# The first norm's shift and scale made by TensorE in column quarters, beside the first three weight tiles

## The reference, cut to what matters

```python
c_act = jax.nn.silu(c)
mod = (c_act @ w_mod[l] + b_mod[l])[:, None, :]
sh1, sc1, g1, sh2, sc2, g2 = jnp.split(mod, N_MOD, axis=-1)
h = rms_norm(x) * (1.0 + sc1) + sh1
proj = h @ w_in[l]
u, v, z, xbc, dt_raw, gate_a, gate_b = jnp.split(proj, offs, axis=-1)
```

## Time and profile before

| | us |
|---|---|
| three runs, median (lowest to highest) | 1546.25 (1546.24 to 1548.23) |
| the profiled execution, own time | 1547.16 |
| its span | 1545.9 |
| TensorE busy with matmuls | 1468.4 |
| VectorE busy | 875.1 |
| ScalarE busy | 636.5 |
| GpSimd busy | 191.0 |
| DMA: moved in all, and mean rate | 142.87 MB, 92 GB/s |
| mean granted clock of TensorE, share of full | 0.983 |

### The profile page before, as it was taken

How to read it: one execution, slowest core, us unless ns; L and a number is a source line. 1 busy time by engine, 2 the same in 40 slices (tenths; PEclk the granted TensorE clock), 3 DMA queues, 4 the chain that set the end, 5 groups by cost and what they waited for, 6 DMA issues and landing times.

```text
span 1545.9 us, 25397 instructions
## 1 busy us (share of the span) xinstructions
PE 1468.4 (95%) x10113; PEld 1154.8 (75%) x10113; DVE 875.1 (57%) x1222; ACT 636.5 (41%) x980; POOL 191.0 (12%) x230
## 2 busy tenths in 40 slices
PE   5899999999999999899998999999998999999996
PEld 2687777777788878688876888888885676766675
DVE  3577777776635754654546442344347765655745
ACT  3564445444555422332234431233324445353433
POOL 0000000000017788630005000000000000000000
PEclk9899999999999999899998999999998999999998
DMA  9332222223245565443332333333332212111111
GB/s 304 82 96 68 69 72 74 75 69 82 68 121 152 155 172 164 126 119 96 95 96 66 98 96 96 95 96 95 97 112 65 56 43 56 43 42 40 49 40 55
DMA packets 263403, 142.87 MB, mean 92 GB/s; under 512 B 4805, under 2 KB 261882, under 8 KB 263290
## 3 DMA queue, kind: packets, MB, share of 16 engines
q1 hardware_dynamic: 263290, 141.26, 32.2%
HBM read 139.14 MB, written 2.10 MB: 91 GB/s over the span
## 4 chain that ended last, share of the span: by engine, by line
PE 85%; DVE 7%; ACT 4%; issue 3%; DMA 0%; SPq 0%; DVEq 0%; ACTq 0%
PE PS L555 24%; PE PS L557 23%; PE PS L556 23%; PE PS L698 1%; DVE Hl L1647 1%; DVE Ww L2248 1%; PE PS L960 1%; PE PS L944 1%; PE PS L662 1%; PE PS L703 1%; DVE macc L1669 1%; PE PS L682 1%; DVE wlo L1635 1%; PE PS L952 1%; PE PS L849 1%
## 5 line engine op out<-in xcount | busy, mean ns | idle before, releaser
L555 PE MATMUL PS<-Hh,whi 128*128 128x512 f32 x1290 | 545.1, 423 | 18.6 <-DVE wlo L1635 3.7
L557 PE MATMUL PS<-Hh,wlo 128*128 128x512 f32 x1290 | 507.9, 394 | 0.0
L556 PE MATMUL PS<-Hl,whi 128*128 128x512 f32 x1290 | 507.3, 393 | 0.0
L1635 DVE TENSOR_TENSOR wlo<-raw,whi 128x1024 fp32r<-128x1024 f32 (+2 forms) x211 | 273.3, 1295 | 106.2 <-ACT whi L1107 104.9
L555 PEld LDWEIGHTS PS<-Hh,whi 128*128 128x128 f32 x1290 | 244.8, 190 | 92.1 <-issue 30.9
L557 PEld LDWEIGHTS PS<-Hh,wlo 128*128 128x128 f32 x1290 | 244.6, 190 | 53.4
L1107 ACT ACTIVATE whi<-raw 128x1024 fp32r<-128x1024 f32 (+2 forms) x211 | 221.5, 1051 | 151.4 <-PE PS L557 151.3
L556 PEld LDWEIGHTS PS<-Hl,whi 128*128 128x128 f32 x1290 | 245.5, 190 | 47.7 <-issue 6.6
L453 POOL TENSOR_TENSOR mbuf<-mbuf,cact 128x1024 f32<-128x1024 f32 x32 | 62.2, 1942 | 468.1 <-DMA mbuf<-in_w_mod_dram 468.1
L555 PE MATMUL PS<-YBh,whi 128*128 128x512 f32 x256 | 99.6, 389 | 0.0
L556 PE MATMUL PS<-YBl,whi 128*128 128x512 f32 x256 | 99.6, 389 | 0.0
(11 more groups left out here) (401 smaller groups left out, 1721.7 us busy)
## 6 DMA issues: line engine op xcount, KB each, us to landing
raw<-in_w_in_dram SPq DMA_DIRECT2D x106, 512.0 KB, 4.0
raw<-in_w_ff_dram SPq DMA_DIRECT2D x64, 512.0 KB, 4.1
mbuf<-in_w_mod_dram SPq DMA_DIRECT2D x32, 512.0 KB, 4.0
wm<-in_w_mod_dram SPq DMA_DIRECT2D x8, 1024.0 KB, 11.9
raw<-in_w_branch_ssm_dram SPq DMA_DIRECT2D x16, 512.0 KB, 4.2
raw<-in_w_out_dram SPq DMA_DIRECT2D x10, 512.0 KB, 4.1
raw<-in_w_branch_gm_dram SPq DMA_DIRECT2D x8, 512.0 KB, 4.1
raw<-in_w_out_dram SPq DMA_DIRECT2D x6, 448.0 KB, 3.8
```

Source lines behind the costliest of these rows:

```text
L555: pe.matmul(bank[:, :], whi[s][:, k, :], xh[:, kk, :], start=kk == 0, stop=False)
L556: pe.matmul(bank[:, :], whi[s][:, k, :], xl[:, kk, :], start=False, stop=False)
L557: last = pe.matmul(bank[:, :], wlo[s][:, k, :], xh[:, kk, :], start=False, stop=t == end - 1 and k == (order or range(kt))[-1])
L1635: v.tensor_tensor(wlo[s][:, 0:kt, :], raw[s][:, 0:kt, :], whi[s][:, 0:kt, :].bitcast(F32), ALU.subtract).then_inc(s_wlo, 1)
```

## The change

VectorE's part in the product of silu(c) and w_mod goes, and so does the second turn of x. In its place:

- SP loads x0 and x1 ahead of `fill1`, x2 and x3 behind it; then the w_mod pieces in quarters, each a piece of the scale and one of the shift (wm4 and wm0, then wm5 and wm1, and so on), with the first three weight tiles and `fill2` between the quarters. Tiles 3 to 5 are loaded ahead of bc and bsb.
- TensorE turns x chunk by chunk as it lands, into eight banks; VectorE copies it to XT (`x_copy`). The reciprocal root is spread over the partitions by four matmuls (L618 of the changed kernel).
- Each piece is multiplied by eight matmuls that write 32 partitions each, four groups in turn (`mod_rows`), copied by ScalarE (`mod_row`), and summed and turned by two matmuls of one column with `selc`, a column that picks one row of each group (`mod_sums`).
- A quarter gives scale and shift of two slices k: VectorE makes the two columns (`h_cols`), then XT by scale by spread root (`h_scaled`), ScalarE adds the shift and rounds (`h_hi`), VectorE takes the rest (`h_lo`).
- Between the quarters TensorE runs tiles dt, cv0 and cv1 for the slices that are there (`part`), so the three tiles are worked by channels, not one after the other.
- After them tile cv2 comes first in `gemm`. The work of `conv` is one tile later than before: conv(0) runs beside cv2, conv(1) beside cv3, conv(2) and conv(3) beside z0 and z1, both gates beside cv4 (`FIRST`, `after`). `dt_steps` runs from cv2 on, so it has four tiles and a rest, where it had six.

The diff, cut to its core:

```diff
 def sp_program(sp):
-        for to, ap in fill1:
-            sp.dma_start(to, ap).then_inc(s_par, 16)
-        for c in range(NC):
-            sp.dma_start(xnat[:, c, :], ...).then_inc(s_x, 16)
-        for i in range(8):
-            sp.dma_start(wm[i][:, :, :], cols(W_MOD, i * 256, 256)).then_inc(s_wm[i], 16)
-        for t in range(3):
-            load(t)
+        load_x(0)
+        load_x(1)
+        for to, ap in fill1:
+            sp.dma_start(to, ap).then_inc(s_par, 16)
+        load_x(2)
+        load_x(3)
+        load_mod0(0)
+        load(0)
+        load(1)
+        load_mod0(1)
+        load(2)
         for to, ap in fill2:
             sp.dma_start(to, ap).then_inc(s_par2, 16)
+        load_mod0(2)
+        load_mod0(3)
+        for t in range(3, 6):
+            load(t)
         sp.wait_ge(s_pc, 5)
...
 def pe_program(pe):
+        def mod_rows(n):
+            if n >= 3:
+                pe.wait_ge(s_mrow, n - 2)
+            pe.wait_ge(s_wm[MOD0[n]], 16)
             for k in range(KT):
-                tr = pe.matmul(row[0:1, 0:256], cact[:, k:k + 1], wm[i][:, k, :], start=k == 0, stop=k == KT - 1)
+                q = 32 * (k % 4)
+                ms = pe.matmul(BK[3 + n % 3][q:q + 32, 0:256], cact[:, k:k + 1].to_broadcast([P, 32]), wm[MOD0[n]][:, k, :],
+                               start=k < 4, stop=k >= 4)
+            ms.then_inc(s_mt, 1)
+        def mod_sums(n):
+            pe.wait_ge(s_mrow, n + 1)
+            if n >= 2 and n % 2 == 0:
+                pe.wait_ge(s_modc, n)
             for j in range(2):
-                ms = pe.matmul(bk[...], macc[:, j * 128:(j + 1) * 128], ones[:, 0:1],
+                ms = pe.matmul(BK[6][:, 2 * n + j:2 * n + j + 1], mrow[n % 2][:, j * 128:(j + 1) * 128], selc[:, 0:1],
                                start=True, stop=True)
+            ms.then_inc(s_ms, 1)
+        def part(t, *ks):
+            ...
+            for k in ks:
+                pe.wait_ge(s_hi, k + 1)
+                pe.wait_ge(s_lo, k + 1)
+                pe.matmul(bank[:, :], whi[t][:, k, :], Hh[:, k, :], start=k == 0, stop=False)
+                pe.matmul(bank[:, :], whi[t][:, k, :], Hl[:, k, :], start=False, stop=False)
+                last = pe.matmul(bank[:, :], wlo[t][:, k, :], Hh[:, k, :], start=False, stop=k == KT - 1)
+        mod_rows(0)
+        mod_rows(1)
+        mod_sums(0)
+        mod_sums(1)
+        part(0, 0, 1)
+        part(1, 0, 1)
+        mod_rows(2)
+        mod_rows(3)
+        mod_sums(2)
+        mod_sums(3)
+        part(0, 2, 3)
+        part(1, 2, 3)
+        mod_rows(4)
+        mod_rows(5)
+        part(2, 0, 1)
+        mod_sums(4)
+        mod_sums(5)
+        part(2, 2, 3)
+        mod_rows(6)
+        mod_rows(7)
+        part(0, 4, 5)
+        mod_sums(6)
+        mod_sums(7)
+        part(1, 4, 5)
+        part(2, 4, 5)
         pe.wait_ge(s_par2, N_PAR2)
...
+        for t in range(3):
+            part(t, 6, 7)
...
 def dve_program(v):
+        def h_scaled(m):
+            v.wait_ge(s_modc, 2 * (m // 2) + 1)
+            ...
+            v.scalar_tensor_tensor(out=tmp[m % 3][:, :], in0=XT[:, m, :], scalar=opc[:, m:m + 1], in1=BK[7][:, :],
+                                   op0=ALU.mult, op1=ALU.mult).then_inc(s_hb, 1)
+        def h_lo(m):
+            ...
+            v.scalar_tensor_tensor(out=Hl[:, m, :], in0=tmp[m % 3][:, :], scalar=modc[:, m:m + 1],
+                                   in1=Hh[:, m, :].bitcast(F32), op0=ALU.add, op1=ALU.subtract).then_inc(s_lo, 1)
+        for j in range(4):
+            h_cols(j)
+            h_scaled(2 * j)
+            h_scaled(2 * j + 1)
+            if j == 0:
+                lo(0)
+            if j == 1:
+                lo(2)
+            h_lo(2 * j)
+            if j == 0:
+                lo(1)
+            h_lo(2 * j + 1)
...
-        for g in range(8):
+        for name, beside in FIRST:
+            main[0] = after(beside, conv, gate_z)
+            tile_steps(name, KT, 5)
+        main[0] = after([("z", 0), ("z", 1)], conv, gate_z)
+        drain()
+        side[0] = ssd(0)
+        for g in range(1, 8):
```

More of the change, by code:

```diff
@@ L219, in build_program @@
     N_BC, N_WS, N_W2 = N_PAR2 + 64, N_PAR2 + 80, N_PAR2 + 128
[L220 removed]
+    s_const, s_par, s_par2 = sem("s_const"), sem("s_par"), sem("s_par2")
+    s_x = [sem(f"s_xl{c}") for c in range(NC)]
     s_wm = [sem(f"s_wm{i}") for i in range(8)]
@@ L272, in build_program @@
     turn(("dt", 0), s_dta, 1)
+    dtT = BK[5]
+    MOD0 = [i for j in range(4) for i in (4 + j, j)]
     for q in range(32):
@@ L372, in build_program, with after @@
     DT, AA, CU, NCU, EC, WE, EL, SC = (dts[:, i, :] for i in range(8))
+    FIRST = [(("cv", 2), [("cv", 0)]), (("cv", 3), [("cv", 1)]), (("z", 0), [("cv", 2)]), (("z", 1), [("cv", 3)])]
+    def after(names, conv, gate_z):
+        gens = [conv(i) if kind == "cv" else gate_z(i) for kind, i in names]
+        for k in range(KT):
+            for gen in gens:
+                next(gen, DONE)
+            yield
     def sp_program(sp):
@@ L404, in sp_program @@
         mod_after = {tile0[name] + 2: q for q, name in enumerate(MODS)}
-        for t in range(3, NT):
+        for t in range(6, NT):
             load(t)
@@ L563, in gemm, with x_turned @@
             return bank
+        def x_turned(c):
+            pe.wait_ge(s_x[c], 16)
+            for m in range(KT):
+                if c == 2 and m == KT - 1:
+                    pe.wait_ge(s_pc, 3)
+                tr = pe.transpose(BK[m][:, c * 128:(c + 1) * 128], xnat[:, c, m * 128:(m + 1) * 128], ident[:, :])
+                if c == NC - 1:
+                    tr.then_inc(s_xtt, 1)
         pe.wait_ge(s_const, 2)
+        x_turned(0)
+        x_turned(1)
         pe.wait_ge(s_par, 16 * 7)
-        pe.transpose(BK[1][:, :128], pr[1][:, :], ident[:, :]).then_inc(s_pt, 1)
@@ new lines, in pe_program @@
+        x_turned(2)
+        x_turned(3)
+        pe.wait_ge(s_xrs, 1)
+        pe.wait_ge(s_xt0, 1)
+        for c in range(NC):
+            ms = pe.matmul(BK[7][:, c * 128:(c + 1) * 128], small[:, 4 + c:5 + c].to_broadcast([P, P]), ident[:, :],
+                           start=True, stop=True)
+        ms.then_inc(s_xsp, 1)
+        pe.wait_ge(s_cact, 1)
+        pe.wait_ge(s_const, 13)
+        pe.wait_ge(s_xt0, 8)
+        def mod_rows(n):
+            if n >= 3:
+                pe.wait_ge(s_mrow, n - 2)
+            pe.wait_ge(s_wm[MOD0[n]], 16)
+            for k in range(KT):
+                q = 32 * (k % 4)
+                ms = pe.matmul(BK[3 + n % 3][q:q + 32, 0:256], cact[:, k:k + 1].to_broadcast([P, 32]), wm[MOD0[n]][:, k, :],
+                               start=k < 4, stop=k >= 4)
+            ms.then_inc(s_mt, 1)
@@ L727, in pe_program @@
         ALL = range(KT)
-        pe.wait_ge(s_pc, 5)
-        gemm(("dt", 0), Hh, Hl, 0)
         side[0] = dt_steps()
         for g in range(8):
-            for j in range(4):
+            for j in range(0 if g else 2, 4):
                 gemm(("cv", 4 * g + j), Hh, Hl, None, ALL)
@@ L1878, in tile_steps @@
                     slot(name)
-        slot(("dt", 0))
+        slot(("cv", 0))
+        slot(("cv", 1))
         side[0] = dt_steps()
-        for g in range(8):
+        for name, beside in FIRST:
+            main[0] = after(beside, conv, gate_z)
+            tile_steps(name, KT, 5)
+        main[0] = after([("z", 0), ("z", 1)], conv, gate_z)
+        drain()
+        side[0] = ssd(0)
+        for g in range(1, 8):
             for j in range(4):
```

194 lines of the change are left out of this document (87 added, 107 removed).

## The result

| | before | changed |
|---|---|---|
| median of four runs each (lowest to highest), us | 1547.24 (1546.24 to 1548.69) | 1530.38 (1528.91 to 1533.54) |
| span of the profiled execution, us | 1545.9 | 1529.7 |
| first matmul of cv2, us | 77.35 | 60.00 |
| first decay matmul of the scan (`maskb`, L648 before, L723 now), us | 101.5 | 86.5 |
| TensorE, VectorE, ScalarE busy, us | 1468.4, 875.1, 636.5 | 1460.0, 868.0, 628.5 |

The ratio is 0.9892, with a 95% interval of 0.9873 to 0.9911: faster by 1.1%, about 17 us. The forecast was 1531.3 us, from 1524.5 to 1539.

What follows compares the result with a forecast made beforehand. TensorE was taken as the bound, 85% of the chain of waits, its head held by VectorE's sums. cv2 from 77.35 to 60.2 us gains 17.15, less 2.2 given back, is 14.95: median 1531.3 us, range 1524.5 to 1539.

Steps and rivals of the forecast that it cites:

- Start: Opening of the kernel: x loaded first, turned and copied, so XT is ready at 16.5 us.
- The groups: Eight matmuls of `mod_rows` in four groups of 32 partitions run at once: 0.85 us, 1.7 at the lower clock.
- Rival 4: Groups in `mod_rows` don't run at once: eight matmuls cost 3.41 us, 20.5 us more in all, 1551.8 us; chance 0.04.
- The quarters: Head's four w_mod quarters at the upper clock: 10.6, 9.4, 8.4 and 8.1 us, plus 0.6 for dt's copy.
- Clock: TensorE at 1.2 GHz for all of quarter 0 and the first half of quarter 1: 5.6 us charged.
- Rival 2: TensorE's clock stays low in the head: cv2 begins at 75.6 us, 1546.7 us in total; chance 0.03.
- Rival 1: TensorE's clock stays up in the head: cv2 begins at 54.6 us, 1525.7 us in total; chance 0.17.
- Entering and leaving the groups: Switching TensorE into and out of the 32-partition groups stretches starts by 0.1 to 0.2 us; 1.0 us in all.
- Transfers: w_mod's quarters land at 16, 23.4, 31.2 and 37.3 us, before they are needed: costs nothing, about 4 us left.
- Behind the head: From cv2 on, TensorE waits 1.8 us for dt's columns and 0.4 at the scan's first state: 2.2 us back.
- Rival 3: VectorE becomes the bound behind the head: 4.5 us given back if bsb is late, 1533.6 to 1536 us; chance 0.13.
- The sum: Whole kernel: 17.15 us gained, 2.2 given back, 14.95 net; 1532.2 us for the profiled execution, median 1531.3.

Runs made afterwards that it cites:

- e1: Changed kernel with each piece's eight matmuls over the whole array one after the other, not in four groups: 1549.39 us.
- e3: Changed kernel with ten unused float32 matmuls of 512 columns put into TensorE's rests in the head: 1526.23 us.
- e2: Changed kernel with tiles dt, cv0 and cv1 run one after the other after the last quarter, no slices between quarters: 1535.43 us.
- e4: Changed kernel with the next quarter's pieces multiplied ahead of this quarter's slices on TensorE: 1527.0 us.
- e8: e7 with the row of bsb on a semaphore of its own: 1528.44 us.
- e7: e4 with five unused matmuls put into TensorE's rests: 1528.33 us.
- e5: e2 with ten unused matmuls of 512 columns in TensorE's rests between the pieces: 1535.38 us.

## Why the prediction was right

*Start* (XT ready at 16.5 us): 16.3. VectorE's copy of a slice from PSUM, which no row of before had, took 0.61 us (four in 2.48 and four in 2.45 us), so 4.9 for eight, as taken.

*The groups* (0.85 us for eight matmuls, 1.7 at the lower level): in quarter 2 two pieces take 1.86 us from their start (42.17) to the next start (44.03), 0.93 each; in quarter 0, at the lower level, 3.57 us (16.56 to 20.13), 1.79 each. Rival 4 is out by this row, and by e1 its price is confirmed. The step was a single row of three groups and 128 columns carried over to four and 256, and it held.

*The quarters.* Full-clock sums plus what was charged for the clock, against the rows: quarter 0 10.6 + 3.7 = 14.3, measured 14.48 (16.56 to 31.04 us); quarter 1 9.4 + 1.9 = 11.3, measured 11.13; quarter 2 8.4, measured 9.06 (42.17 to 51.23 us); quarter 3 with the last copy 8.1 + 0.6 = 8.7, measured 8.77 (51.23 to 60.00 us). With e3's full clock the first three are 10.8, 9.6 and 9.1 us against 10.6, 9.4 and 8.4: good to 0.2 us but for quarter 2. There the prediction added up VectorE's operations between two pieces, and the row for 44 to 50 us shows TensorE busy for 6.00 of 6.00: the slices in waiting had become the longer of the two. The prediction's items for quarters 0 and 1 add up to 10.7 and 9.55, and those for AA's readiness to 13.7, where it wrote 10.6, 9.4 and 13.9; none of these slips matters.

*Clock* (5.6 us, all of quarter 0 and the first half of quarter 1): e3 puts it at 5.3. The amount was right and its place only roughly. The timeline has quarter 1's pieces and sums at the full clock (1.93 and 1.18 us) and the low stretch behind its wait for VectorE, 0.73 in the window from 38 to 44 us: the second half, not the first. As in the earlier trace rows, it falls behind a rest and comes back after a busy stretch, and so part of a rest's price is paid by the work behind it. Rival 2, the rule of the Trainium skill (TensorE: Matmul & The Clock Gate, section on HAM oscillation) that a kernel falls back at each wait between bursts, came true for the two waits in quarters 0 and 1, and was escaped where slices had come thick, from 42 us on. Rival 1, the clock up throughout, didn't happen by itself; e3 shows what it is worth, 54.7 us at cv2 where the rival had 54.6, and 1526.2 us where it had 1525.7.

*Entering and leaving the groups* (1.0 us) was the step furthest off, and little hung on it. In quarter 2 the starts at the entry stand 0.32 us apart (41.85 to 42.17) where slices have 0.23 and e1, which enters no groups, has 0.23 and 0.24 (52.11 to 52.34, 62.67 to 62.91). So an entry costs 0.1 us, and there are four. At the exit the first two starts stand 0.34 us apart (44.03 to 44.37), but they do so behind `mod_sums` too, which uses the whole array (0.32 us, 46.33 to 46.65), and behind the pieces of e1 (0.41 us, 59.06 to 59.47). So no price of the exit is shown, and the prediction read one into the earlier trace rows. Some 0.4 us of the 1.0 are borne out. Over the four quarters measured less forecast leaves 0.7 us (0.2, -0.2, 0.7, 0.1), mostly quarter 2's, and that the two misses nearly cancel is luck. The Trainium skill (TensorEngine Tiling (Array Packing), Key Properties) says that such a change drains TensorE; the entry agrees, the exit doesn't show it, and the drain is no reason against the change.

*Transfers* (nothing): right for the changed kernel, in which TensorE never waits for w_mod. The landing times were too early, though. The rate was taken as 346 GB/s, and the windows from 14 to 44 us have 297 to 350, 319 in the mean. Where a wait for a quarter's second piece ends, that piece has landed: 25.3 to 26.9 us for quarter 1 (e2, e4, e8), 34.5 to 35.4 for quarter 2 (e7, e8, e2), 40.8 and 41.5 for quarter 3 (e5, e2), against 23.4, 31.2 and 37.3. At the full clock (e3) these pieces are wanted at 28.2, 37.8 and 43.5 us. So what is left before the transfers show is 1 to 3 us, not 4, and that is why pieces multiplied ahead come up against them at once.

*Behind the head* (2.2 us): 17.35 at cv2 less 15.0 at the decay matmul is 2.4, and that the two agree is luck. The step had TensorE wait 1.8 us for the columns and the row says 1.4. The 0.4 us at the scan's first state didn't come: behind the start of cv2 TensorE has no other wait up to 104 us. And the turn of dt's result, which costs 0.6 us (from 61.26 to 62.28 us, 1.02, where two slice starts alone need 0.46), now stands behind cv2 and not ahead of it; the prediction has it in TensorE's 12.1 us but not in what is given back. The remaining 0.3 to 0.4 us are wider starts at cv2 and at L703. VectorE's first step was to be 2.5 us behind cv2 and was 2.8, for bc and bsb landed 7.1 us after the issue (55.71 to 62.81 us) and not 5.9. The term of the landing was 1.2 us short, and an issue 4.3 us ahead of cv2 in place of 3.4 made up 0.9 of it. From that step AA took 10.8 us (62.81 to 73.59 us), against 11.4. Rival 3 asked for 4.5 us there and didn't come.

*The sum.* 1532.2 us were forecast for an execution like the profiled one, 1530.9 was measured: 14.95 forecast against 16.3, of which 1.2 us came in the late stage where nothing was changed. By the medians 1531.3 stands against 1530.38; but the forecast started from 1546.25 and the four runs of before have 1547.24, so the gain was 16.9 us and the term short by 1.9, of which the start hides 1.0. The spread of one and the same kernel (1524.28 to 1531.81 us for e8) is in no term of the sum, only in the 3.1 us that the chances go by; it is larger than that, and as large as some of the rivals.

## What to carry to other kernels

A reduction over few rows that a slow engine does beside TensorE can be TensorE's own, if the matmuls write 32 partitions each and run four at a time: here the whole gain hung on the groups (19.9 us at cv2, e1) and 4.6 us of 17.35 on the overlap (e2). Where TensorE's work is cut into quarters that wait for another engine, ask in each rest whether the next piece's transfer is there already and can be worked on; e4 got 5 us by moving lines alone, without an extra instruction. When two ways of filling the same rests are on offer, ask what the engine will wait for once both are in, before adding their gains: here it was the transfers.
